# Two weight sums of a seven-product block made by accumulating transfers, and the low pass of two products joined to the high one

## The reference

```python
D_MODEL, SEQ, D_FF = 1024, 512, 2816

def swiglu(h, w_in, w_out):
    gu = h @ w_in
    gate, up = gu[..., :D_FF], gu[..., D_FF:]
    return (jax.nn.silu(gate) * up) @ w_out

# in each layer i
f = swiglu(rms_norm(h, norm_pre[i, 0]), w_ffn_in[i, 0], w_ffn_out[i, 0])
h = h + FFN_RES_WEIGHT * rms_norm(f, norm_post[i, 0])
# the token mixer, then a second FFN of the same form
```

## Time and profile before

| what | value |
|---|---|
| three executions | 1767.3, 1768.26, 1771.15 us (median 1768.26) |
| profiled execution | 1766.83 us, span 1765.0 us |
| TensorE | busy 1747.9 us, 99% of the span |
| VectorE | busy 1330.9 us, 75% |
| ScalarE | busy 832.1 us, 47% |
| GpSimd | busy 31.1 us, 2% |
| granted TensorE clock, mean of the span | 0.997 |
| chain of waits | TensorE 97%, of it line L866 35% |
| DMA | 183.22 MB, mean 104 GB/s |

### The profile page before, as it was taken

How to read it: one execution, slowest core, us unless ns; L and a number is a source line. 1 busy time by engine, 2 the same in 40 slices (tenths; PEclk the granted TensorE clock), 3 DMA queues, 4 the chain that set the end, 5 groups by cost and what they waited for, 6 DMA issues and landing times.

```text
span 1765.0 us, 31047 instructions
## 1 busy us (share of the span) xinstructions
PE 1747.9 (99%) x12746; PEld 1569.6 (89%) x12753; DVE 1330.9 (75%) x1918; ACT 832.1 (47%) x1389; POOL 31.1 (2%) x63
## 2 busy tenths in 40 slices
PE   9999999999999999999999999999999999999999
PEld 7899899887588899899888998999887988998998
DVE  6899488589758897497588974975888788974964
ACT  5445255355835455255354552553424544552552
POOL 0000000023000000000000000000000000000000
PEclk9999999999999999999999999999998999999999
DMA  6343223322032333223323332332355323322331
GB/s 203 108 131 109 95 96 120 116 70 83 2 108 70 114 116 108 95 97 114 102 72 119 109 108 95 103 114 95 113 165 137 97 82 109 121 96 96 112 105 48
DMA packets 74438, 183.22 MB, mean 104 GB/s; under 512 B 23712, under 2 KB 30512, under 8 KB 74304
## 3 DMA queue, kind: packets, MB, share of 16 engines
q1 hardware_dynamic: 72128, 179.02, 31.5%
q0 software_dynamic: 1600, 1.52, 0.3%
q10 hardware_dynamic: 576, 0.79, 0.1%
HBM read 174.35 MB, written 6.29 MB: 102 GB/s over the span
## 4 chain that ended last, share of the span: by engine, by line
PE 97%; DVE 1%; issue 1%; ACT 1%; DMA 0%; ACTq 0%; SPq 0%; DVEq 0%
PE bank L866 35%; PE bank L525 16%; PE bank L526 16%; PE bank L527 16%; PE bank L618 4%; PE bank L623 2%; PE bank L1025 1%; PE bank L959 1%; PE bank L903 1%; PE bank L927 1%; PE bank L552 1%; PE bank L544 1%; PE bank L942 0%; PE bank L565 0%; PE bank L592 0%
## 5 line engine op out<-in xcount | busy, mean ns | idle before, releaser
L525 PE MATMUL bank<-a_hi,w_hi 128*128 128x512 f32 (+1 forms) x912 | 334.7, 367 | 1.1 <-issue 1.1
L526 PE MATMUL bank<-a_lo,w_hi 128*128 128x512 f32 (+1 forms) x912 | 332.9, 365 | 0.0
L527 PE MATMUL bank<-a_hi,w_lo 128*128 128x512 f32 (+1 forms) x912 | 332.7, 365 | 0.0
L1170 ACT ACTIVATE w_hi<-w_raw 128x1024 fp32r<-128x1024 f32 x192 | 202.7, 1058 | 198.4 <-DVE w_raw L1546 160.8
L866 PE MATMUL bank<-x_hi,w_hi 128*128 128x256 f32 x1024 | 290.1, 283 | 0.0
L866 PE MATMUL bank<-x_lo,w_hi 128*128 128x256 f32 x1024 | 289.7, 283 | 0.0
L866 PE MATMUL bank<-x_hi,w_lo 128*128 128x256 f32 x1024 | 289.6, 283 | 0.0
L1538 DVE TENSOR_TENSOR w_lo<-w_raw,w_hi 128x1024 fp32r<-128x1024 f32 x192 | 234.6, 1222 | 27.3 <-ACT w_hi L1170 26.4
L1526 DVE TENSOR_TENSOR w_lo<-w_raw,w_hi 128x1024 fp32r<-128x1024 f32 x142 | 173.7, 1223 | 90.7 <-ACT w_hi L1119 90.3
L1119 ACT ACTIVATE w_hi<-w_raw 128x1024 fp32r<-128x1024 f32 x142 | 146.6, 1052 | 197.4 <-PE bank L527 184.7
L866 PE MATMUL bank<-raw_forms_hi,w_hi 128*128 128x256 f32 x768 | 215.8, 281 | 3.2 <-ACT sum_sq L1302 3.2
(11 more groups left out here) (245 smaller groups left out, 2912.2 us busy)
## 6 DMA issues: line engine op xcount, KB each, us to landing
w_raw<-stream SPq DMA_DIRECT2D x312, 512.0 KB, 3.3
h_resid<-xT SPq DMA_DIRECT2D x8, 256.0 KB, 6.0
qT<-stream SPq DMA_DIRECT2D x8, 256.0 KB, 6.1
u_scratch<-V SPq DMA_DIRECT2D x8, 256.0 KB, 2.7
a_lo<-u_scratch SPq DMA_DIRECT2D x8, 256.0 KB, 3.0
qT<-z_scratch SPq DMA_DIRECT2D x8, 256.0 KB, 3.6
outT<-h_resid SPq DMA_DIRECT2D x10, 128.0 KB, 1.8
z_scratch<-kT SPq DMA_DIRECT2D x2, 256.0 KB, 4.2
```

What stands on the lines that cost most here:

```text
L525: nc.tensor.matmul(out, lw[0], lx[0], start=first, stop=False)
L526: nc.tensor.matmul(out, lw[0], lx[1], start=False, stop=False)
L527: return nc.tensor.matmul(out, lw[1], lx[0], start=False, stop=last)
L1170: nc.scalar.activation(units_to(w_hi, pair, split), units_from(pair, split), ACT.Copy).then_inc(s_uhi, 1)
```

## The change

On GpSimd's queue, two transfers for each of the 64 pairs add weight blocks out of the stream in DRAM onto blocks already in the ring (`accum_op=ALU.add`): the first onto block 1, once the pair's first slot is loaded, the second onto block 0, once VectorE has done the low part of split 0. VectorE's sum of 1024 columns goes; its two of 512 become additions, the first of which waits for the second transfer. ScalarE's split 1 waits for both. In UP5 and UP3 the passes (high, high) and (high, low) become one matmul of 512 columns over both halves of the bank, and VectorE adds the upper half in instructions of its own (`first_up_lo`, `second_up_lo`). Split 0 of pair i+2 moves ahead of `second_up` of pair i on VectorE, and ahead of the copy after UP7 on ScalarE. In the last pair of a group the copy after UP7 moves ahead of `a_hi_of`. Signs in the x forms and in the ups are turned to match.

```diff
+            def added_blocks(index):
+                for pair in range(first_pair(index, 1), first_pair(index + 1, 1)):
+                    at = FAST_AT[pair]
+                    pool.wait_ge(s_raw[at % RING], 16 * (at // RING))
+                    pool.dma_start(raw_block(pair, 1), stream[at + 1, :, 0:UNIT], accum_op=ALU.add
+                                   ).then_inc(s_t3[pair % 2], 16)
+                    pool.wait_ge(s_ulo, SPLITS * pair + 1)
+                    pool.dma_start(raw_block(pair, 0), stream[at, :, UNIT:2 * UNIT], accum_op=ALU.add
+                                   ).then_inc(s_t1[pair % 2], 16)
...
+                        if product in (UP5, UP3):
+                            whole = bank[Z_BANKS[pair % 2]].rearrange("p (s n) -> p s n", s=2)
+                            nc.tensor.matmul(whole, w[0], both_parts(product)[:, :, k, :],
+                                             start=(product == UP5 and k == 0), stop=(k == KD // 2 - 1),
+                                             skip_group_check=True)
+                            last = nc.tensor.matmul(out, w[1], form(0, product)[:, k, :], start=False,
+                                                    stop=(k == KD // 2 - 1), skip_group_check=True)
+                            continue
...
             def units_hi(pair, split):
-                if split:
-                    act.wait_ge(s_usum, 3 * pair + split)
+                if split == 1:
+                    act.wait_ge(s_t1[pair % 2], 16 * (pair // 2 + 1))
+                    act.wait_ge(s_t3[pair % 2], 16 * (pair // 2 + 1))
+                if split > 1:
+                    act.wait_ge(s_usum, 2 * pair + split - 1)
...
-                    if more_pairs:
+                    if i == 0:
                         pair_loaded(ahead)
-                        if i:
-                            act.wait_ge(s_up, multiplied(pair - 1, UP2))
-                        else:
-                            act.wait_ge(s_mm, n0 - 1)
+                        act.wait_ge(s_mm, n0 - 1)
                         units_hi(ahead, 0)
...
-                    if i:
+                    if more_pairs:
+                        if i:
+                            a_hi_of(i - 1)
+                        if i < FAST - 2:
+                            pair_loaded(ahead + 1)
+                            act.wait_ge(s_up, multiplied(pair, UP2))
+                            units_hi(ahead + 1, 0)
+                        seen_of(pair, UP7, 2)
+                    else:
+                        seen_of(pair, UP7, 2)
                         a_hi_of(i - 1)
-                    seen_of(pair, UP7, 2)
...
             def unit_sums(pair):
-                both = raw[:, 2 * (pair % 2):2 * (pair % 2) + 2, :].rearrange("p a n -> p (a n)")
-                dve.wait_ge(s_ulo, SPLITS * pair + 1)
-                nc.vector.tensor_tensor(both[:, 0:2 * UNIT], both[:, UNIT:3 * UNIT], both[:, 0:2 * UNIT], ALU.subtract
+                dve.wait_ge(s_t1[pair % 2], 16 * (pair // 2 + 1))
+                nc.vector.tensor_tensor(third_sum[:, :], raw_block(pair, 0), raw_block(pair, 2), ALU.add
                                         ).then_inc(s_usum, 1)
-                dve.wait_ge(s_usum, 3 * pair + 1)
-                nc.vector.tensor_tensor(third_sum[:, :], raw_block(pair, 2), raw_block(pair, 0), ALU.subtract
+                dve.wait_ge(s_usum, 2 * pair + 1)
+                nc.vector.tensor_tensor(raw_block(pair, 3), third_sum[:, :], raw_block(pair, 3), ALU.add
                                         ).then_inc(s_usum, 1)
...
                 def second_up(pair):
...
-                                            seen[2][pair % 2], ALU.add).then_inc(s_up2, 1)
+                                            seen[2][pair % 2], ALU.subtract).then_inc(s_up2hi, 1)
+
+                def second_up_lo(pair):
+                    dve.wait_ge(s_up2hi, pair + 1)
+                    to = U[:, pair % 2, HALVES[1]]
+                    nc.vector.tensor_tensor(to, bank[Z_BANKS[pair % 2]][:, T // 2:T], to, ALU.add).then_inc(s_up2, 1)
...
                 for i in range(FAST):
                     pair, ahead = pair0 + i, pair0 + i + 1
                     more_pairs = i < FAST - 1
+                    if i == 0:
+                        units_lo(ahead, 0)
+                    if not more_pairs:
+                        down_lo(n0, 0)
+                    if i:
+                        second_up_lo(pair - 1)
                     if more_pairs:
-                        units_lo(ahead, 0)
                         unit_sums(ahead)
                         units_lo(ahead, 1)
-                    else:
-                        down_lo(n0, 0)
                     first_gate(pair)
                     if i:
                         first_up(pair - 1)
                     if more_pairs:
                         units_lo(ahead, 2)
+                    if i:
+                        first_up_lo(pair - 1)
+                        product(pair - 1)
+                    if more_pairs:
+                        units_lo(ahead, 3)
                     else:
                         down_lo(n0 + 1, 1)
                     if i:
-                        product(pair - 1)
-                    if more_pairs:
-                        units_lo(ahead, 3)
-                    if i:
                         a_lo_of(i - 1)
+                    if i < FAST - 2:
+                        units_lo(ahead + 1, 0)
                     second_up(pair)
+                second_up_lo(pair)
                 first_up(pair)
+                first_up_lo(pair)
                 product(pair)
```

More of the change, by code:

```diff
@@ L312, in build_program @@
         s_usum = sem("weight_blocks_summed")
+        s_t1 = [sem(f"first_weight_sum{i}") for i in range(2)]
+        s_t3 = [sem(f"third_weight_sum{i}") for i in range(2)]
         s_uhi, s_ulo = sem("weight_form_hi"), sem("weight_form_lo")
@@ L378, in form, with both_parts @@
             return (x_hi, x_lo)[part][:, at:at + KD // 4, :].rearrange("p a (b n) -> p (a b) n", b=2)
+        def both_parts(product):
+            at = (FORM_OF[product] - 3) * KD // 4
+            return x_parts[:, :, at:at + KD // 4, :].rearrange("p s a (b n) -> p s (a b) n", b=2)
         block = ctx.enter_context(nc.Block())
@@ L1156, in pair_steps @@
                 if chunk == 4:
-                    form_hi(q // KF, UP4, 1, HALVES[1], -1.0)
+                    form_hi(q // KF, UP4, 1, HALVES[1])
                 act.wait_ge(s_evac, n + 1)
@@ L1175, in pair_loaded, with form_hi @@
                     act.wait_ge(s_raw[at % RING], 16 * (at // RING))
[L1177 removed]
+            def form_hi(index, product, half, tok):
                 act.wait_ge(s_xn, KD * index + KD // 2 * (half + 1))
[L1180 removed]
+                nc.scalar.activation(form(0, product), x_block_of(half, tok), ACT.Copy).then_inc(s_fhi, 1)
             def sum_forms(n0, index):
@@ L1561, in form_lo @@
                 hi, of = form(0, product).bitcast(F32), x_block_of(half, tok)
[L1562 to L1567, removed]
+                nc.vector.tensor_tensor(form(1, product), of, hi, ALU.subtract).then_inc(s_flo, 1)
             def normalised_x(sub, k):
@@ L1787, in first_up, with first_up_lo @@
                     nc.vector.tensor_tensor(U[:, pair % 2, HALVES[0]], bank[Z_BANKS[pair % 2]][:, 0:T // 2],
-                                            seen[1][pair % 2], ALU.add).then_inc(s_up1, 1)
+                                            seen[1][pair % 2], ALU.subtract).then_inc(s_up1hi, 1)
+                def first_up_lo(pair):
+                    dve.wait_ge(s_up1hi, pair + 1)
+                    to = U[:, pair % 2, HALVES[0]]
+                    nc.vector.tensor_tensor(to, bank[Z_BANKS[pair % 2]][:, T // 2:T], to, ALU.add).then_inc(s_up1, 1)
                 def second_up(pair):
```

19 lines of the change are left out of this document (11 added, 8 removed).

## The result

The changed kernel takes **1929.73 us** (median of 4 runs, 1926.63 to 1932.24) against 1767.86 for the kernel before, run in between: ratio **1.0911, 95% interval 1.0899 to 1.0924**, 162 us slower. The forecast was +88 us with a range up to +196: the direction and the mechanism held, and the loss was nearly double the forecast.

A forecast was written before the change was run, and what follows sets the result against it. TensorE, 99% busy, was taken as the bound; VectorE's loop through the landing would replace it: 56 x 3.3 - 96.6 - 3.4 + 4 x 0.7 = +87.6 us on 1766.83, median 1855.8 us, range 1790 to 1964.

The forecast's parts named there:

- The loop: VectorE's in-order work from landing to next issue, plus the landing: 8.14 us + D a pair, against TensorE's 9.9.
- D: Time from issue to landing of the transfer onto block 0: taken as 3.3 us, bounds 1.8 and 5.1.
- the rows' slope: Cost of bytes from profiled plain loads: 3.0 ns a KB, so a plain 256 KB would take 2.5 us.
- 4 groups pay what is above: Down projection ahead of a first group: room for D = 2.6 us; the excess, 0.7, is paid 4 times.
- VectorE's arithmetic: A 1024-column sum (1.25 us) out, two 256-column additions (0.34 or 0.46 each) in: near even, by itself hidden.
- Wide products: UP5 and UP3 on TensorE: 11.4 ns less, 512 times, 5.8 us; off the path once the transfer's wait sets the pace.
- The group's end: Last pair: the 0.56 us stall before UP4 goes, about 0.27 remains before UP3; tails gain 3.4 us in all.
- The signs: Profile marks expected: VectorE's sum waits about 49 + 8 times, 1 to 3 us; TensorE about 1.5 us a pair.
- (a): Hidden transfer: D under 1.7 us, TensorE unbroken, 8 us faster, 1760 us; chance 12%.
- (b): Edge: D about 1.8 to 1.9 us, gain and loss cancel, 1766 to 1772 us; chance 5%.
- (c): Slow accumulation: inline addition or two GpSimd transfers in one queue make D over 5.1 us, above 1964 us; chance 9%.
- (d): After TensorE's first stall everything is shifted and the wait is met no more; its chance is in (a).

The follow-up runs named there:

- the plain run: Changed kernel with the transfer onto block 0 a plain 256 KB copy on GpSimd's queue, its addition left out: 1891.1 us, one run.

## Why the prediction was right in kind and too small

**The loop** was right: of the 12.23 us shown above, VectorE's part is 7.93 (138.11 to 146.04) against 8.04 by the prediction's steps. To the issue it takes 0.28 instead of 0.05, so the loop is 12.23 - 3.98 = 8.25 + D, not 8.14 + D.

**D** is the term that was mis-sized: 4.1 at the median where the prediction took 3.3. The step that failed is "as many bytes read as that 512 KB load: I take D = 3.3". With 4.1 in its place the recorded sum gives 56 x 4.1 - 100 + 4 x 1.5 = +136 in place of +88, which is 48 of the 74 us that were missing. The range held the result because its upper end was taken from the row of 5.1 us. The experiments show what it missed: a plain 256 KB transfer on GpSimd's queue already takes 3.5 and not the 2.5 of the rows' slope, and the addition puts 0.6 on it. The Trainium skill, "DMA: Bandwidth & Descriptors", in its section on loads issued by GpSimd, led to an estimate of 3.8, and 28 us more than forecast. The page's figures are for plain loads: the plain run's 3.5 lies 0.3 below that estimate and 1.0 above the slope's 2.5, and the accumulating form's 4.1 lies 0.3 above it, so the page was nearer than the rows' slope.

**The sum, by groups.** From the starts of L1583, of L515 and of each group's first matmul, means of the eight groups:

| from ... to | predicted with D = 3.3 | measured | more, over 8 groups |
|---|---|---|---|
| group's first matmul to the sums of pair 1 | 5.43 us | 7.61 (8.4 to 9.1 in a first group of an FFN, 6.3 to 6.5 in a second) | 17.4 - 2.8 = 14.6 us |
| sums of pair 1 to those of pair 2 | 10.11 | 11.87 | 14.1 |
| one steady loop (5 in a group) | 11.44 | 12.41 | 38.6 |
| sums of pair 7 to UP7 of pair 6 | 4.03 | 4.03 (187.55 to 191.58) | 0 |
| UP7 of pair 6 | 1.43 | 1.76 (1.50 in six groups, 2.34 and 2.70 in two) | 2.6 |
| pair 7 to the group's last matmul | 12.93 (13.35 before, less 0.42) | 13.22 (13.11 in six, 13.75 and 13.35 in the same two) | 2.3 |

That is 72 of the 74 us by which the forecast fell short (2.8 is what it had set aside for the four first groups); the rest lies outside the groups. Over half is D and the issue in the steady loop. The second row is D too: the landing that it contains took 4.5 to 5.85 us, mean 4.85. It runs beside the loads of a group's start, and that this makes it longer is likely but not shown. The first row is the step "4 groups pay what is above": where the sums of pair 0 wait 3.65 us in the down projection, split 0 of pair 1 starts at 108.26 and not at 106.62, and its transfer is issued at 109.77. The delay reached the next loop in full; I had priced it at 0.7 us, and the first groups are 2.4 us longer than the second ones in this row. The last two rows hold the low clock at two group ends, 3 us, which the prediction had at nothing.

**VectorE's arithmetic**: right that it is hidden in the steady loop, and more so than argued; two additions fewer per pair changed nothing there. At a group's start it is not hidden once the transfers are gone (the stall of 0.39 us). **Wide products**: eight blocks of one wide and one narrow matmul start 0.353 us apart against 0.357 for three narrow ones (3 x 0.1191), a gain of 4.4 ns and not 11.4; the two-run right-hand side that no row showed costs 7 ns. Right that it is off the path. **The group's end**: the stall of 0.56 us was real, and moving the copy alone gives 3.9 us. The stall ahead of UP3 that the prediction put at 0.27 us is there too, 0.49 - 0.12 = 0.37 in every group. **The clock**: the prediction said that it stays at the 2.4 GHz level; it doesn't. That cost about 3 us, at two group ends. **GpSimd's issues at nothing**: 0.85 us each, and VectorE waits for them as a part of D. **The signs**: the sums wait for a landing 64 times, 3.7 us each, where it said about 57 times and 1 to 3 us; TensorE waits 2.0 us and not 1.5; VectorE is 65% busy in the stretch, under the 85% named.

**The rivals.** (a) fell: D is 4.1, not under 1.7. (b), an edge near 1770, fell with it. (c), over 1964, fell too; of its reasons, two GpSimd transfers in one queue are excluded by the run in which D stayed 4.1 without the other one. A slower addition exists, but it is 0.6 us. Whether the 512 KB load beside the transfer makes D longer was not tried. (d) fell: the wait is met 64 times of 64.

## What to carry to other kernels

When work is moved from an engine to a transfer, write down the loop: what orders the transfer, what waits for it on the same in-order queue, and how much other work stands between the two. If loop plus landing is above the bound's period, the excess is paid in every turn, however idle the DMA engines are, and taking arithmetic off the engine doesn't help. Here a transfer with 0.9 us of cover replaced a 1.25 us instruction that was hidden, and cost 162 us. Moving the order for it earlier gives back most of it, until the next loop of the same kind (here the second slot's load) comes up; so list all transfers whose order comes from the loop. And a small stall at the edge of a stage that nobody waits for inside the loop was the one thing to be had: nearly 4 us for moving one copy.

## What the runs showed of the hardware that was not expected

- A 256 KB transfer from GpSimd's queue onto SBUF lands in 3.5 us plain and 4.1 accumulating (medians from the start of the issue); of the 0.6 us between them 0.3 is the issue. 32 KB accumulating still take 2.4, so by an estimate from these two sizes over half of D does not depend on bytes.
- GpSimd needs 0.85 us to issue the accumulating form (0.55 the plain one) and starts 0.28 us after VectorE's instruction ended.
- A plain 256 KB transfer from SP's queue, ordered behind a 512 KB load there, lands in 4.6 us, later than the 3.5 on GpSimd's queue.
- 9 filler matmuls a pair raise the granted clock from 0.972 to 0.988 and don't shorten the time: a low clock behind a wait is a symptom where the next wait absorbs it. It costs 1.5 us where a group ends at it.
- A right-hand side of two runs of 256 columns takes about 7 ns more than one of 512 contiguous ones (0.353 - 0.1191 = 0.234 against 0.2267).
